# Last norm's second half: one square root on ScalarE and two reciprocals on VectorE in place of logarithm and exponential

## The reference

```python
def rms_norm_2(x, g):
    xf = x.astype(jnp.float32)
    y = xf * lax.rsqrt(jnp.mean(xf * xf, axis=-1, keepdims=True) + EPS)
    return (y * g.astype(jnp.float32)).astype(x.dtype)

def second_block(...):
...
        h = h + jnp.einsum('bse,ed->bsd', y, w_out[l])
    return rms_norm_2(h, norm_out_g)
```

## Time and profile before

| | us |
|---|---|
| median of 3 runs | 1711.77 |
| lowest and highest of them | 1711.1 and 1713.98 |
| the profiled execution: its own time | 1712.45 |
| its span, first to last instruction | 1710.7 |
| PE busy in the span | 1666.8 (97%) |
| DVE busy | 1279.3 (75%) |
| ACT busy | 726.9 (42%) |
| POOL busy | 540.0 (32%) |

### The profile page before, as it was taken

One profiled execution on the slowest core, in us unless ns is written; L12 is line 12 of the kernel. 1 busy time (PEld: TensorE's weight loads), 2 busy tenths in 40 slices (PEclk: granted clock), 3 DMA queues, 4 the chain that ended last, 5 costly groups with the idle time before them and its releaser, 6 DMA issues.

```text
span 1710.7 us, 21819 instructions
## 1 busy us (share of the span) xinstructions
PE 1666.8 (97%) x8119; PEld 1376.3 (80%) x8119; DVE 1279.3 (75%) x1556; ACT 726.9 (42%) x933; POOL 540.0 (32%) x409
## 2 busy tenths in 40 slices
PE   7999999999999999999999999999999999999997
PEld 5888888887788888887888877788878788878885
DVE  8987888435677777777775799878888377789764
ACT  7211113225556655566622423411124667673203
POOL 4344544332201011110022323335345322216531
PEclk9999999999999999999999999999999999999999
DMA  6022125141010111101432354112227611344432
GB/s 230 25 75 75 41 91 213 62 166 44 25 38 1 37 38 37 37 2 38 158 121 99 109 182 153 64 68 80 75 85 200 248 50 62 124 154 166 172 111 99
DMA packets 51321, 164.93 MB, mean 96 GB/s; under 512 B 6272, under 2 KB 6912, under 8 KB 50960
## 3 DMA queue, kind: packets, MB, share of 16 engines
q1 hardware_dynamic: 50928, 163.01, 26.9%
q10 hardware_dynamic: 288, 0.52, 0.1%
HBM read 122.49 MB, written 41.03 MB: 96 GB/s over the span
## 4 chain that ended last, share of the span: by engine, by line
PE 80%; DVE 13%; ACT 3%; issue 2%; DMA 1%; SPq 0%; POOL 0%; DVEq 0%; POOLq 0%; ACTq 0%
PE pair L1212 27%; PE pair L1737 9%; PE pair L1399 9%; PE pair L1473 9%; PE pair L1536 5%; PE aux L1509 4%; PE pair L1522 3%; PE pair L1223 2%; PE pair L1287 1%; PE pair L1903 1%; DVE stat_b L2995 1%; PE pair L1231 1%; PE aux L1688 1%; PE aux L1649 1%; PE pair L1888 1%
## 5 line engine op out<-in xcount | busy, mean ns | idle before, releaser
L1046 POOL CAST w_hi<-w_raw 128x1024 fp32r<-128x1024 f32 x66 | 81.2, 1230 | 755.3 <-issue 564.8
L1048 POOL TENSOR_TENSOR w_lo<-w_raw,w_hi 128x1024 fp32r<-128x1024 f32 x66 | 171.2, 2595 | 5.3
L1212 PE MATMUL pair<-op_hi,w_hi 128*128 128x512 f32 x446 | 139.0, 393 | 0.2 <-DVE op_lo L2632 0.2
L1212 PE MATMUL pair<-op_lo,w_hi 128*128 128x512 f32 x446 | 138.0, 391 | 0.0
L1212 PE MATMUL pair<-op_hi,w_lo 128*128 128x512 f32 x446 | 137.8, 390 | 0.0
L2210 ACT ACTIVATE pt_hi<-pair 128x1024 fp32r<-128x1024 f32 x60 | 61.6, 1027 | 128.1 <-issue 84.4
L2627 DVE TENSOR_TENSOR pt_lo<-pair,pt_hi 128x1024 fp32r<-128x1024 f32 x60 | 73.5, 1224 | 53.6 <-ACT pt_hi L2210 50.0
L1473 PE MATMUL pair<-opb_hi,w_hi 128*128 128x512 f32 x256 | 101.9, 398 | 1.1 <-DVEq L185 0.6
L1212 PEld LDWEIGHTS pair<-op_hi,w_hi 128*128 128x128 f32 x446 | 83.6, 188 | 20.9 <-issue 1.6
L1473 PE MATMUL pair<-opb_hi,w_lo 128*128 128x512 f32 x256 | 100.2, 391 | 0.0
L1473 PE MATMUL pair<-opb_lo,w_hi 128*128 128x512 f32 x256 | 99.8, 390 | 0.0
(11 more groups left out here) (544 smaller groups left out, 4415.2 us busy)
## 6 DMA issues: line engine op xcount, KB each, us to landing
w_raw<-weight_units SPq DMA_DIRECT2D x106, 512.0 KB, 4.4
xa<-x_t SPq DMA_DIRECT2D x15, 512.0 KB, 7.6
x_dram<-xa SPq DMA_DIRECT2D x8, 512.0 KB, 6.4
xc<-x_dram SPq DMA_DIRECT2D x8, 512.0 KB, 8.4
x_dram<-xc SPq DMA_DIRECT2D x8, 512.0 KB, 2.8
u_dram<-u_rows SPq DMA_DIRECT2D x8, 512.0 KB, 5.7
c_dram<-c_rows SPq DMA_DIRECT2D x8, 512.0 KB, 2.7
t_raw<-x_dram SPq DMA_DIRECT2D x4, 1024.0 KB, 5.6
```

Source lines behind the costliest of these rows:

```text
L1046: pool.tensor_copy(w_hi[:, half, :], w_raw[:, u % RAW, :]).then_inc(w_hi_done, 1)
L1048: pool.tensor_tensor(w_lo[:, half, :], w_raw[:, u % RAW, :], w_hi[:, half, :], ALU.subtract).then_inc(w_split, 1)
L1212: mm = pe.matmul(acc[:, cols], w, x[:, kx, cols], start=(first and k == 0 and n == 0), stop=(last and k == KT - 1 and n == 2))
```

## The change

ACT's logarithm and two exponentials of the second half become one square root of mean + eps, written to `rstd_f`; the one-column activation ahead of it is a square root as well. DVE gets two instructions, ahead of its five products: the reciprocal of `rstd_f` into `factor`, and the reciprocal of `rstd_f` in place. POOL waits for the second of them (count 29 of `acc_ready`, which (KT - 1) * 3 + KT is) where it waited for ACT's last exponential.

```diff
@@ POOL's program
             pool.wait_ge(copied, LAST_COPY)
-            pool.wait_ge(rstd_ready, 7)
+            pool.wait_ge(acc_ready, (KT - 1) * 3 + KT)
             for k in POOL_LAST:
                 pool.tensor_tensor(xf[:, k, HALF:S], xf[:, k, HALF:S], rstd_f[:, HALF:S], ALU.mult).then_inc(pool_out, 1)
@@ ACT's program
                     norm_rstd(5, aux[:, cols], rstd_f[:, cols])
-                    norm_ahead()
+                    link(act.activation(ln_ahead[:, :], eps_col[:, :], ACT.Sqrt, bias=eps_col[:, :]))
                     for k in POOL_LAST:
...
                     half_square(KT - 1, half)
                     act.wait_ge(stat_done, 6)
-                    link(act.activation(sq_f[:, 0, cols], aux[:, cols], ACT.Ln, bias=eps_col[:, :], scale=1.0 / D))
-                    link(act.activation(factor, sq_f[:, 0, cols], ACT.Exp, scale=-0.5), rstd_ready)
-                    link(act.activation(rstd_f[:, cols], sq_f[:, 0, cols], ACT.Exp, scale=-0.5), rstd_ready)
+                    link(act.activation(rstd_f[:, cols], aux[:, cols], ACT.Sqrt, bias=eps_col[:, :], scale=1.0 / D),
+                         rstd_ready)
@@ DVE's program
             dve.wait_ge(rstd_ready, 6)
+            link(dve.reciprocal(factor, rstd_f[:, HALF:S]))
+            link(dve.reciprocal(rstd_f[:, HALF:S], rstd_f[:, HALF:S]), acc_ready)
             for k in range(KT):
                 if k not in POOL_LAST:
```

## The result

| | us |
|---|---|
| before, median of 20 runs | 1712.04 (1708.93 to 1714.02) |
| changed, median of 20 runs | 1716.38 (1714.08 to 1718.96) |
| ratio, with its 95% interval | 1.0028 (1.0022 to 1.0034) |
| span of the profiled execution | 1714.9 (1710.7 before) |

The changed kernel is slower, by 0.28%, which is 4.8 us with an interval from 3.8 to 5.8.

What follows compares the result with a forecast made beforehand. It took the serial end chain, with POOL's start setting the end, as the bound; two reciprocals of 3.25 us less 2.05 gave +4.45 on 1711.77, 1716.2 us (+0.26%), range 1711.0 to 1719.2.

Steps and rivals of the forecast that it cites:

- The sum: Whole kernel: the shift of +4.45 us added to the median 1711.77 gives 1716.2 us, +0.26%.
- R: Time of one DVE reciprocal of 128x512, two on the path; taken as 3.25 us, 2.8 to 3.9 given 0.43.
- eight passes for each element: Rival on DVE's reciprocals: eight steps of 1.04 ns an element, 4.42 us each, shift +6.8, 1718.6 us; chance 0.25.
- full rate: Rival on DVE's reciprocals: they stream like ordinary work, 0.69 us each, shift -0.67, 1711.1 us; chance 0.22 including up to 1.2.
- the fourth entry of the list: DVE's reciprocal: two elements cost 6 ns over the addition, 3 each; 2.23 us, shift +2.4; chance 0.06 up to 2.7.
- One reading beside it: DVE's short rows of 158, 160 and 169 ns were said to show the long rows' slope of 1.04 ns an element.
- ACT and the table load: ACT's second-half path shrinks from 3.27 to 0.69 us; the 1.28 us load moves to the one-column activation and costs nothing.
- the forecast formula: POOL's start at the second half's products shifts by twice one reciprocal's time less 2.05 us; zero at 1.03 us.
- So POOL still sets the end, and the shift above is that of the whole kernel.: Kernel end: SP issues tile 5 0.03 us after POOL's third product, tile 7 0.34 us after DVE made it.
- Contention: DVE's and POOL's final products, now starting within 0.1 us of each other, cost nothing more; POOL's 3.71 us already holds it.
- R = 1.18: DVE's reciprocal: the 2 ns step from one element to two taken as the slope, 0.16 + 1.02 us, shift +0.3.

Runs made afterwards that it cites:

- e9: Changed kernel with reciprocals of 1 to 1024 elements a partition appended on DVE; 166 ns at two, 3353 at 512, 6.25 ns an element, 12.5 a pair.
- e4: Changed kernel with POOL's reciprocal first (into sq_f) and DVE's second; 1715.37 against 1711.51 us for the kernel before, ratio 1.0028.
- e5: e4 with ACT instead of SP issuing the stores of POOL's three tiles; 1712.94 against 1711.6 us for the kernel before, ratio 1.0013.
- e2: Changed kernel with two products of 128x512 in place of the two reciprocals; 1710.12 against 1711.51 us for the kernel before, ratio 0.9996.
- e3: Changed kernel with one reciprocal, in place, DVE and POOL both reading rstd_f in SBUF; 1714.48 against 1711.51 us for the kernel before, ratio 1.0021.
- e8: e7 with ACT issuing the stores of tiles 3, 4 and 5; 1712.45 against 1711.6 us for the kernel before, ratio 1.0006.
- e7: Changed kernel with second-half sums laid across partitions, root and reciprocal of 128x4, PE spreading the result back; 1713.3 against 1711.6 us before, ratio 1.0006.
- e10: Changed kernel with one reciprocal, in SBUF, copied by ACT to factor in PSUM for DVE; 1713.99 against 1712.14 us for the kernel before, ratio 1.0009.

## Why the prediction was right

**The price of the reciprocal.** The sum took 10 ns for each pair on top of the ordinary rate, R = 3.25. Measured: 3.36 and 3.35. The mechanism is shown by e9: the time goes by pairs, and a pair costs 12.5 ns. The prediction's pair was 2 x 1.04 + 10 = 12.1. It was read from the earlier trace rows: 10 ns above a multiplication of the same shape, and nothing more for the second element. The rivals of eight passes for each element (R = 4.42) and of full rate (0.69) fell with the measured 3.36.

Part of this is luck. The whole rate hangs on a difference of 10 ns between two short instructions, and the choice of the multiplication as the other one is argued by no more than the same tile: set against the addition of one or two elements (158 and 160 ns) the same reading by pairs gives 6 ns, R = 2.23, which is the fourth entry of the list. The prediction itself gave its reading no more than 0.43. One reading beside it was wrong, though nothing rests on it: 158, 160 and 169 ns for 1, 2 and 8 elements rise by 1.6 ns an element, not by the 1.04 of the long rows.

The Trainium skill, "VectorE: DVE Perf Modes", section "First, the fixed hardware budget", gives Reciprocal a repeat count of 8. That pointed the right way, but it could not be turned into a rate: the measured 12.5 ns for a pair are 12 steps of 1.04 ns.

**ACT and the table load.** As forecast: 0.69 us for the square root, the load ahead of it costs nothing, and POOL starts 0.15 us behind the second reciprocal (1706.89 against 1706.74; 0.14 was put in). DVE's four products delayed the first reciprocal by 1700.00 - 1699.50 = 0.50 us (0.49 forecast, from 1700.51 to 1701.00).

**The sum.** POOL's start moved from 3.40 us behind ACT's first instruction on the sums to 8.08, by 4.68; the forecast formula gives 2 x 3.36 - 2.05 = 4.67. This is the part that was worked out, and it holds within 0.01.

**The step that failed.** "So POOL still sets the end, and the shift above is that of the whole kernel." The tail grew by 5.21 us, 0.53 more than POOL's start moved. I had let SP's eight stores shift with their makers. e4 showed that POOL's finishing 3.4 us sooner changes nothing, and e5 that three stores taken from SP give 1.8 us: in the changed kernel the end is set by DVE's second product and SP's seven issues behind it, back to back. Before, DVE was 0.7 us ahead of POOL, which kept the stores apart. With DVE only 0.1 us ahead they bunch, and an issue takes up to 0.65 us. The prediction had SP come to tile 7 0.34 us after DVE made it; it was 0.83. The sum of issues has to be worked out as a queue of its own. It would have spoiled the full-rate rival too: e2 is that case, and ends with before.

**The size.** Forecast +4.45 us (+0.26%), measured +0.28% (0.22 to 0.34). R was 0.22 us too low in the sum (twice 0.11), the stores 0.53 us; together they make the 5.2 of the tail. That the difference of the two medians, 4.34 us, lies nearer to the forecast than the tail does is chance: the interval of the ratio, 3.8 to 5.8 us, holds both.

**Contention.** I had costed it between DVE's and POOL's products at nothing, and it was: 3.88 for DVE's five and 3.73 for POOL's three, as before. e3 shows that this hangs on `factor` lying in PSUM, which the prediction did not say.

**Left open.** Why an issue takes 0.33 us alone and 0.65 in a row of eight, no run tells. It mostly goes with how closely the stores follow each other, but the last of e8 took 0.78 with 0.43 us of room before it. Whether the share of the tiles between DVE and POOL could be chosen better for this tail was not tried.

## What to carry to other kernels

Price a DVE reciprocal by its pairs of elements in a partition, 12.5 ns each: it is free for a column and 3.36 us for 512, so a row of 512 that is the same in all partitions is a bad place to divide, and a table load of 1.28 us with two exponentials of 0.6 is cheaper. Short instructions of the same operation in the trace gave the right rate here when set against another operation of the same shape, where their own step from one element to two gave R = 1.18; but at 10 ns the choice of that other operation moves the answer by 1 us, so a ladder of lengths as in e9 is the way to be sure. Before giving PE a short job at the end of a kernel, look at the clock it was granted there: e7's ran at half. At the end of a kernel, lay out the last stores as a queue with the length of each issue; which engine finishes last may not be what sets the end.

## What the runs showed of the hardware that was not expected

- DVE's reciprocal in float32 costs 12.5 ns for each pair of elements of a partition (e9), also into PSUM (3361 ns for 512 in the changed kernel) and from PSUM (3366).
- DVE's product of 128x512 with both tensors in SBUF takes 1.63 us when it starts beside a running POOL product, and 0.75 when it starts first, alone, or with one tensor in PSUM; POOL's takes 1.7 instead of 1.26 (e3, e10). The two need not share a tile (1.62 against 0.69 us in the kernel before).
- The issue of a 256 KB store on SP takes 0.33 us alone and up to 0.65 in a bunch of eight (0.78 once, in e8); the last landing is waited for 1.7 us in e5, 2.4 with the bunch.
- Eight float32 products of 128x128 with as many different weights are 16 passes and take PE 3.78 us at a granted clock of 0.50 (e8), 3.57 with the last two at full clock (e7).
